# Gate counts per token in a one-core mixture block: one float32 product becomes two passes of the rounded float32 type, one-hots move to GpSimd, and the low weight part goes last within a unit

## The reference

```python
q = (xt @ w_query).reshape(T, PEER_HEADS, 2, PEER_HALF)
scores = einsum('thpc,hpnc->thpn', q, sub_keys)
vals, idx = lax.top_k(scores, PEER_TOPK)                 # 16 of 128, for each half
...                                                      # 16 of the 256 sums; i1, i2 are the halves' keys
experts = (i1 * PEER_N_KEYS + i2).reshape(T, 8 * 16)
gates = softmax(top_vals)
u = take(expert_down, experts); hdn = gelu(u . x)
y = sum over the 128 chosen experts of gates * hdn * take(expert_up, experts)
```

## Time and profile before

| | |
|---|---|
| median of three runs | 2976.7 us |
| profiled execution, its own time | 2971.47 us |
| its span, first to last instruction | 2969.7 us |
| TensorE busy | 2873.6 us, 97% |
| VectorE busy | 1877.3 us, 63% |
| ScalarE busy | 1411.6 us, 48% |
| GpSimd busy | 0.2 us |
| DMA | 556.84 MB, 188 GB/s on average |
| mean granted TensorE clock | 0.988 |

### The profile page before, as it was taken

How to read it: one execution, slowest core, us unless ns; L and a number is a source line. 1 busy time by engine, 2 the same in 40 slices (tenths; PEclk the granted TensorE clock), 3 DMA queues, 4 the chain that set the end, 5 groups by cost and what they waited for, 6 DMA issues and landing times. The chain is left out here.

```text
span 2969.7 us, 40225 instructions
## 1 busy us (share of the span) xinstructions
PE 2873.6 (97%) x15510; PEld 2471.8 (83%) x15510; DVE 1877.3 (63%) x3185; ACT 1411.6 (48%) x2025; POOL 0.2 (0%) x4
## 2 busy tenths in 40 slices
PE   8999899999999999999999999997999999999998
PEld 6878787888889988887888888886888888999876
DVE  5556555588988864455555555556667766555555
ACT  4444444344545544444444444445554445444444
POOL 0000000000000000000000000000000000000000
PEclk9999899999999999999999999998999999999999
DMA  6643356555556665566666767764554455555554
GB/s 212 210 149 116 114 170 206 163 192 188 191 194 215 214 210 185 186 192 207 220 210 221 225 220 231 241 208 136 187 167 146 145 164 195 187 187 188 186 169 154
DMA packets 180062, 556.84 MB, mean 188 GB/s; under 512 B 20624, under 2 KB 51616, under 8 KB 176928
## 3 DMA queue, kind: packets, MB, share of 16 engines
q1 hardware_dynamic: 177568, 537.49, 56.2%
q10 hardware_dynamic: 2304, 16.78, 1.4%
HBM read 533.21 MB, written 20.99 MB: 187 GB/s over the span
## 5 line engine op out<-in xcount | busy, mean ns | idle before, releaser
L780 DVE TENSOR_TENSOR wlo<-raw,whi 128x1024 fp32r<-128x1024 f32 (+1 forms) x965 | 1179.8, 1224 | 940.5 <-ACT whi L1376 938.2
L1376 ACT ACTIVATE whi<-raw 128x1024 fp32r<-128x1024 f32 (+1 forms) x965 | 1016.5, 1056 | 976.9 <-PE bank L452 962.8
L452 PE MATMUL bank<-aX,whi 128*128 128x512 f32 (+1 forms) x4000 | 1411.3, 397 | 0.2 <-ACT whi L1376 0.2
L452 PE MATMUL bank<-aX,wlo 128*128 128x256 f32 (+1 forms) x3984 | 1119.1, 281 | 7.4 <-DVE wlo L780 7.4
L452 PE MATMUL bank<-whi,aX 128*128 128x512 f32 x3200 | 992.8, 391 | 6.8 <-DVE aX L783 5.6
L452 PEld LDWEIGHTS bank<-aX,whi 128*128 128x128 f32 (+1 forms) x4000 | 748.4, 187 | 170.1 <-issue 4.3
L452 PEld LDWEIGHTS bank<-aX,wlo 128*128 128x128 f32 (+1 forms) x3984 | 752.7, 189 | 12.1 <-DVE wlo L780 11.5
L452 PEld LDWEIGHTS bank<-whi,aX 128*128 128x128 f32 x3200 | 603.0, 188 | 134.2 <-DVE aX L783 5.9
L452 PE MATMUL bank<-wlo,aX 128*128 128x512 f32 x1600 | 625.4, 391 | 1.0 <-DVE wlo L780 1.0
L452 PEld LDWEIGHTS bank<-wlo,aX 128*128 128x128 f32 x1600 | 301.5, 188 | 64.7 <-DVE wlo L780 2.7
L1376 ACT ACTIVATE aX<-HB 128x256 fp32r<-128x256 f32 x128 | 53.4, 418 | 214.3 <-DVE HB L783 214.3
(11 more groups left out here) (184 smaller groups left out, 1539.6 us busy)
## 6 DMA issues: line engine op xcount, KB each, us to landing
raw<-in_w_down SPq DMA_DIRECT2D x256, 512.0 KB, 3.5
raw<-in_w_up SPq DMA_DIRECT2D x256, 512.0 KB, 3.6
raw<-in_w_in SPq DMA_DIRECT2D x176, 512.0 KB, 3.6
raw<-in_w_out SPq DMA_DIRECT2D x32, 512.0 KB, 3.5
raw<-in_w_pq SPq DMA_DIRECT2D x32, 512.0 KB, 3.5
gate_scratch<-HB ACTq DMA_DIRECT2D x16, 1024.0 KB, 4.8
raw<-in_w_o SPq DMA_DIRECT2D x32, 512.0 KB, 4.3
raw<-in_w_pg SPq DMA_DIRECT2D x32, 512.0 KB, 4.2
```

The lines of the kernel that those rows point to most:

```text
L452: return e.matmul(o, lhsT, rhs, start=start, stop=stop, skip_group_check=True)
L780: e.tensor_tensor(wlo[:, s, 0:n], raw[:, r, 0:n], whi[:, s, 0:n].bitcast(F32), ALU.subtract).then_inc(s_lo, 1)
L1376: return e.activation(o, i, f, **k)
```

## The change

Two edits. First, the one-hots of i1 go into a float32 buffer (`BO`) and those of i2 straight into `AB`, both built by GpSimd, which has a list of its own now. The gates are split into a rounded part `GH` (ScalarE) and a rest `GL` (VectorE). For each batch VectorE multiplies `BO` by `GH` and by `GL`, two operations over all four tokens, in place of eight small ones. TensorE multiplies each token's one-hots of i2 by both, two passes of the rounded type in place of one float32 product. Buffers move, and the last wait of ScalarE's list goes from i = 101 to i = 92. Second, in `group_x` all eight products with `whi` come before the eight with `wlo`, and the wait for `wlo` stands between them.

```diff
@@ buffers
-    JT = hb(25856, 768).rearrange("p (s c) -> p s c", s=3)
-    AB = hb(26624, 2048).rearrange("p (i s c n) -> p i s c n", i=2, s=2, c=4)
+    BO = hb(23552, 1024).rearrange("p (i c n) -> p i c n", i=2, c=4)
+    JT = hb(24576, 512).rearrange("p (s c) -> p s c", s=2)
+    GL = hb(25088, 256)
...
+    GH = alloc(F_, "GH", [128, 256], F32R)
+    AB = alloc(F_, "AB", [128, 2, 3, 4, 128], F32R)
@@ TensorE
         def gate_batch(n):
-            w.wait_ge(s_oh, 8 * n + 8)
+            w.wait_ge(s_oh, 4 * n + 4)
+            w.wait_ge(s_bv, 2 * n + 2)
             b = vacant(GBF[n])
             for c in range(4):
-                last = mm(b[:, c * 128:c * 128 + 128], AB[:, n % 2, 1, c, :], AB[:, n % 2, 0, c, :], True, True)
+                o = b[:, c * 128:c * 128 + 128]
+                mm(o, AB[:, n % 2, 0, c, :], AB[:, n % 2, 1, c, :], True, False)
+                last = mm(o, AB[:, n % 2, 0, c, :], AB[:, n % 2, 2, c, :], False, True)
             last.then_inc(s_gb, 1)
@@ TensorE, group_x
                 w.wait_ge(s_hi, u + 1)
                 for k in range(8):
-                    kt, c = (u - g.first) * 8 + k, slice(k * 128, k * 128 + 128)
-                    ready(kt)
-                    mm(o, whi[:, s, c], aX[:, kt, :], kt == 0, False)
-                    w.wait_ge(s_lo, u + 1)
-                    last = mm(o[:, 256:512], wlo[:, s, c], aX[:, kt, 0:256], False, u == g.end - 1 and k == 7)
+                    ready(k0 + k)
+                    mm(o, whi[:, s, k * 128:k * 128 + 128], aX[:, k0 + k, :], k0 + k == 0, False)
+                w.wait_ge(s_lo, u + 1)
+                for k in range(8):
+                    last = mm(o[:, 256:512], wlo[:, s, k * 128:k * 128 + 128], aX[:, k0 + k, 0:256], False, u == g.end - 1 and k == 7)
                 last.then_inc(s_mm, 1)
@@ VectorE
         def gate_rows(n):
             i = n % 2
-            for fill in JTF:
-                evacuated(fill)
+            w.wait_ge(s_bo, 4 * n + 4)
             if n >= 2:
                 w.wait_ge(s_gb, n - 1)
-            for c in range(4):
-                t = n * 4 + c
-                e.tensor_scalar(AB[:, i, 0, c, :], iota, JT[:, 0, t:t + 1], None, ALU.is_equal).then_inc(s_oh, 1)
-                e.tensor_scalar(AB[:, i, 1, c, :], iota, JT[:, 1, t:t + 1], JT[:, 2, t:t + 1], ALU.is_equal, ALU.mult).then_inc(s_oh, 1)
+            for x, g in ((1, GH[:, :].bitcast(F32)), (2, GL)):
+                tt(AB[:, i, x, :, :], BO[:, i, :, :], g[:, 4 * n:4 * n + 4].unsqueeze(2).to_broadcast([128, 4, 128]), ALU.mult).then_inc(s_bv, 1)
...
             if k == 96:
                 w.wait_ge(s_jt, 1)
-                e.tensor_copy(JT[:, 0:2, :].rearrange("p s c -> p (s c)"), banks[JTF[0][0]]).then_inc(s_free[JTF[0][0]], 1)
-                e.tensor_copy(JT[:, 2, :], banks[JTF[1][0]][:, 0:256]).then_inc(s_free[JTF[1][0]], 1)
+                e.tensor_copy(JT[:, :, :].rearrange("p s c -> p (s c)"), banks[JTF[0][0]]).then_inc(s_free[JTF[0][0]], 1)
+                w.wait_ge(s_gh, 1)
+                tt(GL, banks[JTF[1][0]][:, 0:256], GH[:, :].bitcast(F32), ALU.subtract).then_inc(s_free[JTF[1][0]], 1)
@@ GpSimd, new
+    @block.gpsimd
+    def _(e):
+        w = Gate(e)
+        for b, n in JTF:
+            w.wait_ge(s_free[b], n)
+        w.wait_ge(s_const, 32)
+        for n in range(64):
+            i = n % 2
+            if n >= 2:
+                w.wait_ge(s_bv, 2 * n - 2)
+            for c in range(4):
+                e.tensor_scalar(BO[:, i, c, :], iota, JT[:, 0, 4 * n + c:4 * n + c + 1], None, ALU.is_equal).then_inc(s_bo, 1)
+            if n >= 2:
+                w.wait_ge(s_gb, n - 1)
+            for c in range(4):
+                e.tensor_scalar(AB[:, i, 0, c, :], iota, JT[:, 1, 4 * n + c:4 * n + c + 1], None, ALU.is_equal).then_inc(s_oh, 1)
@@ ScalarE
+                if k == 96:
+                    w.wait_ge(s_jt, 1)
+                    act(GH[:, :], banks[JTF[1][0]][:, 0:256], ACT.Copy).then_inc(s_gh, 1)
...
-            if i == 101:
+            if i == 92:
```

More of the change, by code:

```diff
@@ L147, in _build @@
         sem(n) for n in ("s_mask", "s_lg", "s_mx", "s_ex", "s_cn", "s_rd", "s_ht", "s_ov"))
-    s_spill, s_keys, s_sco, s_top, s_rc, s_gx, s_jt, s_oh, s_gb = (
-        sem(n) for n in ("s_spill", "s_keys", "s_sco", "s_top", "s_rc", "s_gx", "s_jt", "s_oh", "s_gb"))
+    s_spill, s_keys, s_sco, s_top, s_rc, s_gx, s_jt, s_gh, s_oh, s_bo, s_bv, s_gb = (
+        sem(n) for n in ("s_spill", "s_keys", "s_sco", "s_top", "s_rc", "s_gx", "s_jt", "s_gh", "s_oh", "s_bo", "s_bv", "s_gb"))
     s_gw, s_gl = [sem("s_gw0"), sem("s_gw1")], [sem("s_gl0"), sem("s_gl1")]
@@ L227, in _build @@
     E_.close()
+    F_ = ExitStack()
+    alloc(F_, "below_gates", [128, 25344])
+    GH = alloc(F_, "GH", [128, 256], F32R)
+    AB = alloc(F_, "AB", [128, 2, 3, 4, 128], F32R)
+    F_.close()
     C = ExitStack()
@@ L615, in group_x @@
                 s = u % NSPL
+                k0 = (u - g.first) * 8
                 w.wait_ge(s_hi, u + 1)
                 for k in range(8):
-                    kt, c = (u - g.first) * 8 + k, slice(k * 128, k * 128 + 128)
-                    ready(kt)
-                    mm(o, whi[:, s, c], aX[:, kt, :], kt == 0, False)
-                    w.wait_ge(s_lo, u + 1)
-                    last = mm(o[:, 256:512], wlo[:, s, c], aX[:, kt, 0:256], False, u == g.end - 1 and k == 7)
+                    ready(k0 + k)
[3 more added lines that the diff above has]
+                    last = mm(o[:, 256:512], wlo[:, s, k * 128:k * 128 + 128], aX[:, k0 + k, 0:256], False, u == g.end - 1 and k == 7)
                 last.then_inc(s_mm, 1)
@@ L977, in route @@
                 w.wait_ge(s_jt, 1)
-                e.tensor_copy(JT[:, 0:2, :].rearrange("p s c -> p (s c)"), banks[JTF[0][0]]).then_inc(s_free[JTF[0][0]], 1)
-                e.tensor_copy(JT[:, 2, :], banks[JTF[1][0]][:, 0:256]).then_inc(s_free[JTF[1][0]], 1)
+                e.tensor_copy(JT[:, :, :].rearrange("p s c -> p (s c)"), banks[JTF[0][0]]).then_inc(s_free[JTF[0][0]], 1)
+                w.wait_ge(s_gh, 1)
+                tt(GL, banks[JTF[1][0]][:, 0:256], GH[:, :].bitcast(F32), ALU.subtract).then_inc(s_free[JTF[1][0]], 1)
+            if k == 97:
+                evacuated(JTF[1])
             if 97 <= k < 161:
```

## The result

The changed kernel takes **3128.19 us** (median; 3126.38 to 3130.08), beside 2977.59 us for the kernel before on the same chip: a ratio of 1.0502, 95% interval 1.0489 to 1.0514. The forecast was 2968 us, its range ended at 3036. The prediction is wrong: the kernel is 5% slower, and lies 92 us above the range.

The account below looks back on a forecast made before the run. TensorE was taken as the bound, busy 97% of the span and all of the gate stage. Terms -7.7 + 0.6 - 2 = -9 us on 2971.5 gave 2962, plus 5.2 for the median: 2968 us, range 2957 to 3036.

Parts of the forecast that it names:

- GpSimd's term: Gate stage: eight GpSimd comparisons at 0.28 us, 2.24 us of a 3.72 us unit, hidden behind TensorE.
- the shared way: Gate stage: VectorE's two-input work, 2.35 us a unit, shuts GpSimd out of memory; 2997 to 3025 us or more, chance 0.32.
- too slow by itself: Gate stage: a GpSimd comparison costs over 0.465 us, slower; chance 0.07 shared with the narrow product going through in parts.
- the hidden case: Main forecast: GpSimd's gate-stage work hidden behind TensorE and the `wlo` waits gone; 2968 us, chance 0.51.
- Edit one, TensorE's part: Gate stage: eight narrow rounded products at 0.120 us cost 0.96 us a batch against 0.95; +0.6 us over 64 batches.
- the cheap product: Gate stage: the narrow product costs 0.067 us, the stage gains 26 us; 2941 us, chance 0.03.
- the one in parts: Gate stage: the narrow product costs 0.20 us, +43 us; about 3012 us, chance 0.07 shared with GpSimd alone being slow.
- Edit two: `group_x`: `wlo` wanted 1.59 us later, so TensorE's waits for it vanish; -7.7 us, bounds 0 and -8.6.
- the rival in which the waits come back: `wlo` waits: VectorE is as late at the next unit, nothing gained; 2975 to 2978 us, chance 0.07.
- A second speed of the stream: Pairs of products slow from 0.346 to 0.354 us after the gate stage; counted -2 us, +-6 for the range.
- the new order is free: `group_x`: two runs of eight products cost what eight pairs cost, 0.347 against 0.346 us; a unit stays at 2.77 us.
- VectorE easier by 0.6 us, worth nothing: Gate stage: two wide products (1.20 us) replace comparisons (1.80 us) on VectorE; no gain, as TensorE does not wait for it.

Follow-up runs that it names:

- the kernel with VectorE nearly idle: Changed kernel with VectorE's wide gate-stage instructions kept in number, order and waits but cut in width (results wrong); 3039.28 us in one run.
- the bfloat16 run: Changed kernel with no GpSimd, gates in two bfloat16 parts and bfloat16 one-hots all built by VectorE; 2977.29 us, ratio 0.9991.
- the kernel with edit two alone: Kernel before with only `group_x` changed, the eight `wlo` products behind the eight with `whi`; 2974.59 us, ratio 0.9989.
- three of the kernels above: Kernels with all comparisons on VectorE (3003.92 us), with one wide GpSimd subtraction for its four comparisons (2987.41 us), and with bfloat16 counts (2977.29 us).
- the kernel without GpSimd: Changed kernel with all eight comparisons of a unit on VectorE and products in the old pairs; 3003.92 us, ratio 1.0082.

## Why the prediction was wrong

**The failed step** is GpSimd's term, put down as hidden. First its price: "I take 0.28 as nearest: 2.24 us of 3.72, hidden behind TensorE". It was VectorE's price for the same comparison, chosen between 0.033 us (one-element fills) and no upper bound at all. GpSimd's is 0.585 us from start to start, twice that. The estimate of 110 to 280 ns that stood beside the shared way was too low by the same factor or more. Eight are 4.68 us, over the 3.72 that hide them, also with VectorE nearly idle. That alone is 64 x 0.96 = 61 us, and the kernel with VectorE nearly idle shows it (58.6 above its kernel before). So the condition of the rival "too slow by itself" (over 0.465 us), to which I gave 0.07 together with another case, was met.

**The shared way** is the other part: 1.41 us a unit, 90 us, which the forecast put at nothing. The rival had the mechanism and the deciding point (0.17 us), but its two terms were off in opposite directions. It priced a comparison at up to 0.28 us ("more if a comparison costs more" is all it says beyond), and it let VectorE's 2.35 us shut GpSimd out wholly. With 0.585 us and full exclusion a unit would be 2.35 + 4.68 = 7.03 us; measured are 6.09, so 2.35 us of wide work cost GpSimd 1.41 us, 60% of it. The rule of the Trainium skill that I cited (SBUF — State Buffer, Who interferes with whom), that the second to start is blocked until the first is done, is borne out in direction, and both ways (GpSimd's 1.41 us a unit, VectorE's split of 12.63 us), but as a sum of whole durations it overstates: it would have given 64 x 3.31 = 212 us. Why it is 60% was not taken apart: what share of a GpSimd instruction needs what they share stays open. I gave this rival 0.32 and the hidden case 0.51, against a rule in writing, on a price that no row had.

**The two causes add.** They are one list on one engine: its own work and what holds it off. The rival's sum, 2.35 us + 8 prices, had this form; at 0.585 us it gives about 3180 us. But the range stopped at a price of 0.3 us with 0.11 left above it, and "too slow by itself" stood as a case apart, without a time of its own. With no bound on the price from above, there was none on the time.

**Edit one, TensorE's part**: right. 0.119 us a product against 0.120, and nothing gained or lost; the load bounds it, as the bfloat16 run shows. Neither the cheap product nor the one in parts came.

**Edit two**: the wait moved as forecast, but it did not vanish. -7.7 us was taken, -3.3 measured. The waits for `wlo` fell (8.6 to 1.9 us), but "VectorE is behind only for a unit at a time" failed for `QKb` and `DD`: they are the next things TensorE wants from the same late engine, and with `whi` 6.2 of the 6.7 us came back. My bound of 0 named this case, and so, at a chance of 0.07, did the rival in which the waits come back; it put them at the next unit's `wlo`.

**A second speed of the stream**: two runs of eight have one speed. In the kernel with edit two alone, TensorE's timeline ahead of the gate stage, seven units apart:

```profile
699.41 2.00 PE L452 MATMUL bank<-aX,whi 128*128 128x512 f32 x8
...
718.97 2.00 PE L452 MATMUL bank<-aX,whi 128*128 128x512 f32 x8
```

That is 2.79 us a unit, and behind the stage the kernel after takes 1304.30 - 1301.50 = 2.80. Pairs have 2.77 ahead and 2.83 behind the earlier trace rows. So "the new order is free" was off by 0.02 us a unit ahead of the stage, some 3 us over the 128 units of `pq` and `down` there, and the 94 units behind it gave 3 us back: the term of -2 came out near 0. Why pairs have two speeds stays open.

**VectorE easier by 0.6 us, worth nothing**: true as it stood, since it only waited longer. Where VectorE has more to do, or TensorE less, it would count: VectorE was the bound in three of the kernels above.

## What to carry to other kernels

Before work goes to an idle engine, have a price for that instruction on that engine: a probe of a dozen instructions in the old kernel costs one run, and the neighbour engine's row is no price. Then add what the two hold each other off to the price, do not choose between them, and compare with the period of the engine that is to hide it. And when a wait is moved later in the list, look at what else is wanted from the late engine: where its list is the limit, the wait turns up in front of the next operand.

## What the runs showed of the hardware

- A GpSimd comparison with a scalar from memory lasts 0.60 us for 128 columns (0.585 from start to start), 0.44 for 64 and 0.92 for 256; into float32 and into the rounded type it is the same at 128. A copy of 128 columns lasts 0.29, a two-input instruction of 512 columns 1.03. VectorE's comparison of 128 lasts 0.28 (0.20 from start to start, 901.69 to 902.48 us for four in the kernel without GpSimd).
- Beside VectorE's wide work, a GpSimd comparison lasts 0.97 to 1.03 us in the mean. One-input instructions of VectorE held it off too. In the other direction, twelve two-input instructions in a row on GpSimd held one VectorE split for 12.63 us, and one of them beside VectorE's four small comparisons made these 1.31 to 1.65 us long in place of 0.88.
- A product of 128 columns by a 128-column weight costs 0.119 us in the rounded type and 0.054 in bfloat16, start to start; the weight loads last 188 and 98 ns.
- In the stage where TensorE waited some 2 us in front of a batch, the granted clock was 0.84 to 0.87 on average, a mix of its two levels, 1.2 and 2.4 GHz: eight narrow products behind such a wait took 902.90 - 901.26 = 1.64 us in place of 0.95 (the granted clock from 902 to 904 us was 0.50, the lower level). It cost nothing there, as GpSimd set the period. In the kernel with VectorE nearly idle the waits were 0.7 us, and the granted clock stayed at 1.00.
